# Hybrid decoder step on one core: S5's window taps loaded as 10 KB pieces, and a new common order of the mixer's work

## What is computed

```
n1   = rmsnorm(x) @ w_in                       # 1024 -> 512 (u) + 4 x 512 (r, k, v, z)
s5   = gated(S5 state-space mixer of u)        # 32 groups of 16 channels, 64 complex states each
rw   = RWKV-7 mixer of r, k, v, z              # 8 heads of 64
x    = x + concat(s5, rw) @ w_out
x    = x + cross_attention(rmsnorm(x), 256 memory tokens, 4 heads)
x    = x + top-4-of-32 clamped-SwiGLU experts(rmsnorm(x))
y    = rmsnorm(x)                              # and the new states and memory keys and values
```

## Time and profile before

| what | value |
|---|---|
| runs | 1459.82 us median of 3 (1458.54 to 1466.42) |
| the profiled execution | 1459.49 us, of which span 1457.7 us |
| mean granted clock of TensorE | 0.981 of full |
| PE busy | 1369.6 us, 94% of the span |
| VectorE busy | 444.9 us, 31% |
| ScalarE busy | 253.7 us, 17% |
| GpSimd busy | 55.4 us, 4%, 111 instructions |
| largest shares of the chain that ended last | PE 71%, DMA 20%, DVE 7% |
| of that chain, loads of `u_windows` | 2% |

### The profile page before, as it was taken

How to read it: one execution, slowest core, us unless ns; L and a number is a source line. 1 busy time by engine, 2 the same in 40 slices (tenths; PEclk the granted TensorE clock), 3 DMA queues, 4 the chain that set the end, 5 groups by cost and what they waited for, 6 DMA issues and landing times.

```text
span 1457.7 us, 21163 instructions
## 1 busy us (share of the span) xinstructions
PE 1369.6 (94%) x8649; PEld 695.7 (48%) x8649; DVE 444.9 (31%) x881; ACT 253.7 (17%) x480; POOL 55.4 (4%) x111
## 2 busy tenths in 40 slices
PE   8958999999999999999999999998998999988997
PEld 5735688866665633434334343343343433433442
DVE  5699846434121321312112111121121111311112
ACT  3223431212223212101101011011010110110102
POOL 4233000000000000000000000000000000000000
PEclk9978999999999999999999999999999999999999
DMA  8960121013939769999999999999999999999994
GB/s 325 203 116 30 62 91 60 32 60 120 388 135 410 279 252 397 401 423 428 427 428 428 428 428 428 428 428 428 428 428 428 428 428 428 428 429 425 428 426 179
DMA packets 43335, 471.84 MB, mean 324 GB/s; under 512 B 4992, under 2 KB 10368, under 8 KB 11520
## 3 DMA queue, kind: packets, MB, share of 16 engines
q1 hardware_dynamic: 37264, 461.42, 76.4%
q10 hardware_dynamic: 6000, 9.41, 3.3%
HBM read 465.33 MB, written 5.48 MB: 323 GB/s over the span
## 4 chain that ended last, share of the span: by engine, by line
PE 71%; DMA 20%; DVE 7%; issue 1%; ACT 1%; ACTq 0%; SPq 0%; DVEq 0%
DMA big<-in_w_gu 18%; PE bank L1189 16%; PE bank L1238 14%; PE bank L716 10%; PE bank L1112 5%; PE bank L979 2%; PE bank L799 2%; PE bank L1302 2%; PE bank L1258 2%; DMA big<-u_windows 2%; PE bank L898 1%; PE bank L1119 1%; PE bank L1214 1%; PE bank L1287 1%; DVE big L1847 1%
## 5 line engine op out<-in xcount | busy, mean ns | idle before, releaser
L1189 PE MATMUL bank<-big 128*64 128x512 f32 x1920 | 427.9, 603 | 27.6 <-DMA big<-in_w_gu 27.4
L1189 PEld LDWEIGHTS bank<-big 128*64 128x64 f32 x1920 | 147.1, 138 | 305.3 <-issue 295.0
L1238 PE MATMUL bank<-big 128*64 128x512 f32 x960 | 209.4, 594 | 0.0
L716 PE MATMUL bank<-big 128*128 128x320 f32 (+1 forms) x688 | 187.5, 430 | 9.1 <-DVE big L1922 6.8
L716 PEld LDWEIGHTS bank<-big 128*128 128x128 f32 x688 | 130.1, 191 | 63.0 <-issue 13.4
L2242 DVE TENSOR_TENSOR big<-big,bank 128x320 f32<-128x320 f32 x120 | 58.6, 488 | 303.0 <-PE bank L1258 297.8
L2228 DVE TENSOR_SCALAR big<-bank 128x512 f32<-128x512 f32 x32 | 22.2, 693 | 391.5 <-PE bank L1189 361.3
L1238 PEld LDWEIGHTS bank<-big 128*64 128x64 f32 x960 | 70.2, 137 | 127.9 <-issue 126.0
L1593 ACT ACTIVATE big<-big 128x512 f32<-128x512 f32 x30 | 18.8, 626 | 448.4 <-DVE big L2228 448.4
L1353 ACT ACTIVATE big<-bank 128x320 f32<-128x320 f32 (+3 forms) x122 | 53.1, 436 | 232.7 <-PE bank L716 41.9
L1112 PE MATMUL bank<-big 128*128 128x512 f32 x192 | 87.1, 603 | 1.4 <-DVE big L2176 1.4
(11 more groups left out here) (408 smaller groups left out, 1146.5 us busy)
## 6 DMA issues: line engine op xcount, KB each, us to landing
big<-in_w_gu SPq DMA_DIRECT2D x128, 2048.0 KB, 25.1
big<-in_w_down SPq DMA_DIRECT2D x62, 2048.0 KB, 22.3
big<-in_dense SPq DMA_DIRECT2D x47, 1024.0 KB, 8.4
big<-u_windows ACTq DMA_DIRECT2D x32, 160.0 KB, 10.4
big<-in_w_down SPq DMA_DIRECT2D x4, 1024.0 KB, 20.8
big<-in_smw SPq DMA_DIRECT2D x1, 1408.0 KB, 19.3
big<-in_xT SPq DMA_DIRECT2D x2, 640.0 KB, 4.6
big<-in_consts SPq DMA_DIRECT2D x1, 1028.5 KB, 14.5
```

What stands on the lines that cost most here:

```text
L716: last = mm(b[:, 0:n], w[:, k, :], src[:, k, :], start=(k == 0), stop=(k == kt - 1))
L1189: last = mm(ps[n][part, :], xte[:, 2 * j + k, part], w[s][:, k, n * 512:n * 512 + 512], start=False, stop=end)
L1238: last = mm(ps[bank][part, :], actT[:, 4 * d + i, part], w[s][:, i, h * 512:h * 512 + 512], start=(d == 0 and i == 0), stop=end)
```

## The change

Four things are changed.

1. The scratch tensor `u_windows` has rows of 320 values with no zeros between, and the rows are stored so that the same channel of the 8 groups of a tile lies in 8 neighbouring rows. A tap of a tile is then 16 pieces of 8 x 320 values, 10240 bytes, one to a partition. What a shifted piece picks up from the row ahead falls where the mask is zero; seven zeros are stored once ahead of the first row (`front_stored`).
2. The store is made tile by tile (`store_rows`). ScalarE issues the stores of tiles 0 and 1 right behind its sine, then squares the memory tokens, then issues the windows of tiles 0 and 1, each behind the stores of its own tile and the one ahead, and then the stores of tiles 2 and 3. VectorE makes u1 right behind u0. The squares of the memory (`memsq`) move to another region, since window 1's buffer is now filled earlier.
3. `m0` is issued ahead of chunk 12 and not of chunk 6.
4. `MIX_ORDER` is new, and window 1 is masked by ScalarE (seven instructions) and not by VectorE.

```diff
-MIX_ORDER = [("in", "k0"), ("memsum", 0), ("load", 0), ("in", "k1"), ("f", 0), ("in", "k2"), ("load", 1), ("c", 0), ("in", "k3"),
-             ("par", 0), ("memtotal", 0), ("in", "z0"), ("f", 1), ("in", "z1"), ("win", 0), ("win", 1), ("blk", 0), ("memroot", 0), ("load", 2), ("scan", 0),
...
+MIX_ORDER = [("in", "k0"), ("memsum", 0), ("f", 0), ("in", "k1"), ("in", "k2"), ("in", "k3"), ("memtotal", 0), ("par", 0), ("c", 0),
+             ("memroot", 0), ("in", "z0"), ("win", 0), ("blk", 0), ("load", 2), ("f", 1), ("y", 0), ("win", 1), ("scan", 0), ("in", "z1"),
...
-        u_dram = nc.dram_tensor("u_windows", [W5, T + 7], F32)
+        u_dram = nc.dram_tensor("u_windows", [W5 + 1, T], F32)
...
-                if c == 2 * EARLY:
+                if c == 4 * EARLY:
                     sp.dma_start(m0, a["m0"]).then_inc(S("m0_in"), 16)
...
-                if ct < 2:
+                if ct < 1:
                     pe.wait_ge(S("uwin"), ct + 1)
                 else:
-                    pe.wait_ge(S("uwin_places"), (BL - 1) * (ct - 1))
+                    pe.wait_ge(S("uwin_places"), (BL - 1) * (ct - 0))
...
+            def store_rows(ct):
+
+                stored(act, f"u{ct}")
+                to = bass.AP(u_dram, T + ct * P * T, [[T, 8], [8 * T, GC], [1, T]])
+                act.dma_start(to, uT[:, ct, 7:]).then_inc(S(f"u_stored{ct}"), 16)
+
+            def load_windows(ct):
+
+                if ct >= 2:
+                    computed(act, f"loc{ct - 2}")
+                act.wait_ge(S(f"u_stored{ct}"), 16)
+                act.wait_ge(S(f"u_stored{ct - 1}" if ct else "front_stored"), 16)
+                for tap in range(BL):
+                    src = bass.AP(u_dram, T + ct * P * T + tap - 7, [[8 * T, GC], [1, 8 * T]])
+                    act.dma_start(uwins[ct % 2][tap * GC:(tap + 1) * GC].rearrange("p g t -> p (g t)"), src).then_inc(S(f"uwin_in{ct % 2}"), 16)
+
+            act.wait_ge(S("u_pad"), 1)
+            act.dma_start(bass.AP(u_dram, T - 7, [[7, 1], [1, 7]]), uT[0:1, 0, 0:7]).then_inc(S("front_stored"), 16)
+            store_rows(0)
+            store_rows(1)
             act.wait_ge(S("mem_in"), 16)
             for k in range(KT):
                 step(af(memsq[:, k, :], memT[:, k, :], ACT.Square), "memsq")
-            stored(act, "u3")
-            act.wait_ge(S("u_pad"), 1)
-            act.dma_start(u_dram.ap().rearrange("(c p) t -> p c t", p=P), uT).then_inc(S("u_stored"), 16)
+            load_windows(0)
+            load_windows(1)
+            store_rows(2)
+            store_rows(3)
...
-                for tap in range(BL):
-                    src = bass.AP(u_dram, ct * P * (T + 7) + tap, [[T + 7, GC], [GC * (T + 7), 8], [1, T]])
-                    act.dma_start(uwins[ct % 2][tap * GC:(tap + 1) * GC], src).then_inc(S(f"uwin_in{ct % 2}"), 16)
```

26 lines of the change are left out of this document (11 added, 15 removed).

## The result

The changed kernel takes 1439.49 us, the median of four executions (1437.37 to 1441.48); the kernel before took 1460.39 beside it (four, 1458.54 to 1466.42). The ratio is 0.985, 95% interval 0.982 to 0.988: 21 us faster by the medians, 18.0 by the spans of the two profiled executions (1457.7 and 1439.7). The prediction was 1432.0 with a range of 1427 to 1446. Direction and range held. Of the forecast gain of 27.8 us a quarter is missing by the medians and a third by the two profiled executions; the profiled one of the changed kernel (1441.48) was the slowest of its four.

A forecast was written before the change was run, and what follows sets the result against it. PE was taken as the bound ahead of the expert weight stream: 25.8 us of waits and 5.4 of slow clock go, 0.85 and 2.3 come, 28.0; the walk's 27.8 was taken, 1459.8 - 27.8 = 1432.0 us, range 1427 to 1446.

The forecast's parts named there:

- The bound and what can be reached: PE bounds; its reachable waits before the weight stream, 25.8 us, plus 5.4 of slow clock: at most 31.2 us.
- The loads: Window loads on ScalarE's queue: window 0 lands by 41 us, window 1 by 53, both hidden, so zero cost.
- The slow end of the bounds: Rate of the 10 KB window pieces: bounds 141 and 428 GB/s, the 141 of the small pieces taken.
- The order, walked through: Job-by-job timing of the new list up to the bonus sums: they start at 175.5 instead of 203.3, gaining 27.8 us.
- the walk: The same job-by-job timing by semaphore waits and durations; time within 5 us either way, 1428 to 1437, chance 0.60.
- Rival (a): VectorE becomes the bound, waits at output 1 or 2 and bonus sums: 1436 to 1440; shares chance 0.27.
- nothing to spare: Block 1: ScalarE's mask 1 and copies end at 70.6 us, just when output 0 ends, so no wait and no margin.
- rival (b): Window 1 lands late, delaying mask 1 and block 1: gain 24 us or less, 1436 to 1444; shares chance 0.27.
- one of the signs that the prediction named for being wrong: PE idle time at block 1 or 2 released by ScalarE's masks, where the walk's margin was nil.
- the new waits: PE waits the new order adds before the bonus sums: 0.85 us at block 0 and 2.3 at output 1.
- a wait I have overlooked: An unnamed further wait, pooled with rivals of VectorE as bound and late window 1: up to 1448 us, chance 0.27.
- m0's load: Moving m0's load (1 MB) behind chunk 11 costs zero, since its use comes far behind the bonus sums.

The follow-up runs named there:

- e2: Changed kernel with the old scratch layout (rows of 327 values, a tap again 128 pieces of 1,280 bytes): 1442.11 us, ratio 0.9862.
- e4: Changed kernel with projection r2 moved between output 1 and block 2: 1432.85 us, ratio 0.9803.
- e8: Changed kernel with stores of tiles 2 and 3 ahead of the taps, z3 before block 1, r2 before block 2, C1 before scan 1: 1434.24 us.
- e5: Changed kernel with the stores of u's tiles 2 and 3 issued ahead of the 16 tap loads of windows 0 and 1: 1435.60 us.
- e12: Changed kernel with r2 between output 1 and block 2 and the stores of tiles 2 and 3 ahead of the taps: 1432.61 us.
- e7: Changed kernel with m0's load put back behind chunk 6, as in the kernel before: 1443.04 us, ratio 0.9863.
- e9: Changed kernel with 45 extra short matmuls on PE ahead of block 0's wait for its windows: 1435.91 us, ratio 0.9821.
- e11: Changed kernel with 45 extra short matmuls ahead of block 0's wait and stores of tiles 2 and 3 ahead of the taps: 1435.84 us.
- e1: Changed kernel with the window loads of tile 3 issued behind block 2 instead of ahead of r1: 1435.61 us, ratio 0.9815.
- e10: Changed kernel with 65 extra short matmuls on PE ahead of block 0's wait for its windows: 1447.86 us, ratio 0.9910.

## Why the prediction was right, and what it missed

**The bound and what can be reached: right.** All the long waits named (8.64, 8.76 and 6.82 us, and their cause, VectorE's 13.48 for the windows of tile 1) are gone (that of 6.82 stood ahead of v0 and not of r2, as the old list shows: r3 and v0 follow block 2; this changes no sum), and every microsecond gained ahead of the bonus sums was there at the end (18.0 and 18.0).

**The loads: right.** Window 0 was to be issued from 29.0 and land by 41, 11 us ahead of its use; it was issued from 30.19, and mask 0 waited for nothing. The rate was taken as 141 GB/s. Over 38 to 47 the queue moved 1.18 MB, 131 GB/s, in 86% of the engines' time:

```profile
q10 hardware_dynamic: 233, 1.18, 86.0%
```

The slow end of the bounds was the right one: 10 KB pieces aren't faster than small ones by anything like the 428 GB/s of the wide loads, and e2 bears it out. The Trainium skill (SBUF — State Buffer, Door 1: The DMA port swizzle) makes the rate depend on how many ports the partitions reach, 109 GB/s for the four of a tap. The larger pieces brought no gain that a run shows, but the 131 measured lie above that figure.

**The order, walked through: right where only semaphores decide.** Scan 0 was to end at 65 and ended at 64.72. Output 0 started at 68.74 (69.2 forecast) and waited for nothing. At output 1 the walk had 2.3 us for C1, done at 91.3; C1 ran from 80.84 to 89.24: scan 1 was done 1.4 us sooner than forecast, and beside GpSimd's F3 it took 8.4 us, not the 9.1 of the walk. Rival (a), VectorE as the bound, didn't happen in the changed kernel, where VectorE has idle time of 4.26 us at 123; with PE's stops gone it shows at output 2 (0.73 us in e4, 3.41 in e8). Block 1 was said to have "nothing to spare", and 1.28 us is what that cost. The walk had load 2 issued at 57.8; it went out at 59.44, because the walk didn't ask when store 2, behind sixteen taps in one queue, would land. That is rival (b) in small, shown by e5, and one of the signs that the prediction named for being wrong.

**The term that was mis-sized is the new waits.** The walk put the bonus sums at 175.5 and said 175 to 180; they came at 185.31. The measured time lies outside the walk's own 1428 to 1437, in the band that it gave to the rivals and "a wait I have overlooked" (0.27): the range held by the room left for the unknown, not by a rival that described it. The sum had 3.15 us of new waits, both on semaphores. There were 2.5 on semaphores (1.21 and 1.28; none came at output 1), 5.1 at limits of the instruction stream, and 6.1 of slow clock behind the second of these, where the prediction had none and wrote that the granted clock would be near 1.0 from 62 to 150. The new order brings output 1 and block 2 together, 176 matmuls in 4 us; between matmul 616 (93.0) and 747 (96.1) PE had 3.0 us of work, and the piece was there only at 98.99. The old order had parameters 2 and r2 between them, and the same records took 10.1 us (106.8 to 116.93). The one sign of it in the trace before, the 0.23 us inside block 1, was counted as a wait that would go, without asking what it could be, in a loop that waits for nothing. Where that stop is kept away, the forecast time comes out: 1432.9 (e4) and 1432.6 (e12), with the bonus sums at 174.72 and 175.84 for 175.5. That it comes out so closely is in part luck: e4's waits are 0.88, 1.57 (a stop at 486) and 0.73 us, 3.2 in all, and the sum had 3.15 made of 0.85 and 2.3 elsewhere.

**Open.** m0's load was priced at zero; e7 gives 0 to 3.5 us, none of it ahead of the bonus sums. Whether the clock falls behind a stop of 2 to 3 us was not the same from kernel to kernel (0.67 after, 1.00 in e9, 0.92 in e11), so the 6 us are no fixed price of the stop. What sets a piece's time between 3.5 and 9.6 us is argued from single profiles alone. The packets of the stops took 0.9 to 1.8 us themselves and began 0.8 to 7.2 us after the piece ahead was begun, so it is mostly the start of the fetch that varies. In e1, with load 3 out of the way, 616 to the end of the stop took 3.6 us (97.6 to 101.17), in after 6.0, in the kernel before, with nothing else on the DMA engines, 3.5 (82.6 to 86.15). But in e10 a piece also took 3.5 us (76.34 to 79.88) with 0.54 MB of weights moving in 76 to 78, so weights alone don't make it late.

## What to carry to other kernels

When a new order brings small matmul jobs together, count instructions as well as microseconds: a walk by semaphores alone treats an engine's own instructions as free. An idle time inside a loop without waits, however short, is a sign that the stream is at its limit there; a long job between the two short ones (e4) can hide it. Count again after each change, since any added instruction moves the limits (e9, e10). And a store that a later load waits for belongs ahead of the bulk loads in its queue.

## What the runs showed of the hardware

PE's instructions arrive in packets of 16 KB on the queue "q8 instruction", one for 256 records of PE, which is about 127 of the trace's matmuls with their weight loads. At the stops the next was usable 3.5 to 9.6 us after the one ahead was begun, and 1.2 to 1.7 us after its packet was complete. That the other transfers share in the delay is not shown. (A whole execution shows 52 such packets for 17,983 records, fewer than one for each 256, so not every piece has its packet in the trace.)

"Issue" as a releaser hides at least three causes in this case: PE's own instructions late (2.15 inside block 1), ScalarE's copy late (1.28 ahead of it), GpSimd's copies of the start states late (3.41 ahead of output 2 in e8).

A wait of the same length doesn't always cost the same. Behind the wait of 1.78 us at 277 to 287 us, which every kernel has, the same six matmuls took 1.56 us in the changed kernel and 2.93 in e12:

```profile
286.78 1.56 PE L799 MATMUL bank<-big 128*128 128x256 f32 x6 [1.78 <-DVE big L2077]
```

```profile
277.31 2.93 PE L799 MATMUL bank<-big 128*128 128x256 f32 x6 [1.77 <-DVE big L2077]
```

After it the next wait (L799, L2081) comes 6.28 us later in the first and 7.82 in the second. In e10, which took 2.19 there, the granted clock was 0.72 in 286 to 292, and in the changed kernel 1.00. Differences of 1.5 us between two profiles are within what this alone gives.

Short matmuls aren't alike: 128 on 128 rows into four row groups took 10.8 ns each (1.38 us), 90 of 32x32 into one row group 38 ns each.
